# Eight products of the identity with itself, ahead of the first transposes, left out

## What is computed

```python
xn = rmsnorm(h, norm_mix_g)
proj = xn @ w_in
...
log_f = jax.nn.log_sigmoid((f_logit + b_f).astype(jnp.float32))
...
att_o = forgetting_attention(heads(q), heads(k), heads(v), log_f)
conv_o = conformer_conv(glu_in, w_dw, b_dw, ln_g, ln_b)
mixed = jnp.concatenate([att_o, conv_o], axis=-1)
h = h + mixed @ w_out
hn = rmsnorm(h, norm_ffn_g).reshape(B * T, D)
h = h + moe_ffn(hn, w_router, b_router, w_gu, b_gu, w_down, b_down).reshape(B, T, D)
return rmsnorm(h, norm_final_g)
```

## Time and profile before

| what | us |
|---|---|
| median of three executions | 1038.73 |
| lowest and highest | 1037.36, 1039.56 |
| the profiled execution's own time | 1039.37 |
| span of the profiled execution, first to last instruction | 1037.6 |
| TensorE busy | 1009.1 (97% of the span) |
| VectorE busy | 242.2 (23%) |
| ScalarE busy | 163.1 (16%) |
| mean granted TensorE clock | 0.992 |

### The profile page before, as it was taken

One profiled execution on the slowest core, in us unless ns is written; L12 is line 12 of the kernel. 1 busy time (PEld: TensorE's weight loads), 2 busy tenths in 40 slices (PEclk: granted clock), 3 DMA queues, 4 the chain that ended last, 5 costly groups with the idle time before them and its releaser, 6 DMA issues.

```text
span 1037.6 us, 11003 instructions
## 1 busy us (share of the span) xinstructions
PE 1009.1 (97%) x4821; PEld 398.1 (38%) x4822; DVE 242.2 (23%) x532; ACT 163.1 (16%) x303; POOL 15.0 (1%) x28
## 2 busy tenths in 40 slices
PE   9999999999999999999999999998999999999997
PEld 7875534333333333333333333333333333233332
DVE  3995341211011111111111112111111112011112
ACT  6144321111011111111110111010111011001102
POOL 4000000000000000000000000000000000000000
PEclk9999999999999999999999999999999999999999
DMA  9995799999999999999999999999999999999995
GB/s 310 389 421 199 277 340 400 410 416 425 428 425 436 425 435 426 433 427 431 428 436 427 432 429 430 433 431 429 430 431 426 434 429 429 427 428 426 427 421 217
DMA packets 35275, 421.62 MB, mean 406 GB/s; under 512 B 4269, under 2 KB 8665, under 8 KB 15258
## 3 DMA queue, kind: packets, MB, share of 16 engines
q1 hardware_dynamic: 33658, 420.57, 96.7%
q10 hardware_dynamic: 1568, 0.33, 0.2%
HBM read 419.82 MB, written 1.05 MB: 406 GB/s over the span
## 4 chain that ended last, share of the span: by engine, by line
PE 64%; DMA 28%; DVE 6%; ACT 1%; issue 0%; SPq 0%; DVEq 0%; ACTq 0%
PE work L1243 53%; DMA ring<-in_w_gu 24%; PE resid L1243 7%; DVE main L937 4%; DMA ring<-in_w_down 3%; PE work L1551 1%; PE work L1627 1%; DMA main<-in_x 0%; PE work L1581 0%; PE work L1362 0%; PE work L1461 0%; DVE main L944 0%; DVE ring L916 0%; DVE ring L947 0%; DVE main L991 0%
## 5 line engine op out<-in xcount | busy, mean ns | idle before, releaser
L1243 PE MATMUL work<-ring,main 128*64 128x512 f32 (+1 forms) x3080 | 689.0, 597 | 16.9 <-DMA ring<-in_w_gu 15.2
L1243 PEld LDWEIGHTS work<-ring,main 128*64 128x64 f32 (+1 forms) x3080 | 218.9, 138 | 462.3 <-issue 412.0
L1146 DVE TENSOR_SCALAR main<-work 128x512 f32<-128x512 f32 x32 | 22.1, 691 | 555.6 <-PE work L1243 555.6
L777 ACT ACTIVATE main<-main 128x512 f32<-128x512 f32 x32 | 20.2, 631 | 435.8 <-DVE main L1146 435.8
L1243 PE MATMUL work<-ring 128*128 128x256 f32 (+2 forms) x308 | 71.8, 403 | 0.9 <-DVE ring L947 0.8
L1243 PE MATMUL resid<-main 128*128 128x512 f32 (+1 forms) x136 | 68.0, 618 | 0.8 <-ACT main L840 0.8
L1243 PEld LDWEIGHTS work<-ring 128*128 128x128 f32 (+1 forms) x308 | 55.6, 186 | 15.7 <-issue 8.7
L1243 PE MATMUL work<-bgu_rows,ident 128*64 128x512 f32 (+1 forms) x260 | 61.0, 588 | 0.0
L795 ACT ACTIVATE main<-work 64x512 f32<-64x512 f32 x60 | 35.5, 591 | 126.9 <-PE work L1243 126.2
L1139 DVE TENSOR_SCALAR lent<-count,place,gates 128x64 f32<-128x64 f32 x68 | 17.9, 309 | 154.6 <-PE work L1581 146.8
L937 DVE SCALAR_TENSOR_TENSOR main<-ring,main 128x256 f32<-128x256 f32 x116 | 46.6, 478 | 1.3 <-ACT main L651 1.1
(11 more groups left out here) (200 smaller groups left out, 332.3 us busy)
## 6 DMA issues: line engine op xcount, KB each, us to landing
ring<-in_w_gu SPq DMA_DIRECT2D x33, 4096.0 KB, 40.5
ring<-in_w_gu SPq DMA_DIRECT2D x40, 2048.0 KB, 18.2
ring<-in_w_down SPq DMA_DIRECT2D x16, 4096.0 KB, 40.6
ring<-in_w_down SPq DMA_DIRECT2D x13, 2048.0 KB, 16.3
ring<-in_w_down SPq DMA_DIRECT2D x23, 1024.0 KB, 29.0
ring<-in_w_gu SPq DMA_DIRECT2D x7, 3072.0 KB, 35.8
ring<-in_w_gu SPq DMA_DIRECT2D x20, 1024.0 KB, 24.9
ring<-in_w_down SPq DMA_DIRECT2D x4, 3072.0 KB, 37.4
```

The source lines that it names most:

```text
L777: nc.scalar.activation(sig_h, gate_h, ACT.Sigmoid, scale=SWIGLU_ALPHA).then_inc(sig_ready, 1)
L1146: V.tensor_scalar(gate_h, work[:, GATE_BANK, :], SWIGLU_LIMIT, None, ALU.min).then_inc(gate_clamped, 1)
L1243: return nc.tensor.matmul(out_, lhsT, rhs, start=start, stop=stop, skip_group_check=True)
```

## The change

Both calls of `keep_warm` and the helper are left out. The eight products of `open_resid`, the transpose of `mix_rows` and everything after it stay, in the same order and with the same waits.

```diff
-            def keep_warm(n, out_):
-
-                for _ in range(n):
-                    mm(out_, ident[:, :], ident[:, :], True, True)
-
             pe.wait_ge(ident_ready, 1)
             def open_resid():
...
             open_resid()
-            keep_warm(3, work[:, 0, 0:P])
             pe.wait_ge(mix_in, 16)
             nc.tensor.transpose(work[:, 3, 0:KB], mix_rows, ident[0:KB, 0:KB]).then_inc(vecs_turned, 1)
-            keep_warm(5, work[:, 0, 0:P])
```

## The result

The changed kernel takes 1040.98 us, the median of nine executions (1039.97 to 1043.06); the kernel before, run beside it, 1038.60 (nine, 1037.17 to 1039.56). The ratio is 1.0028, 95% interval 1.0017 to 1.0038: slower, by 2.4 us in the medians. The forecast was 1040.5, inside 1038.5 to 1043.0. Of its three outcomes it had "the same" as the likeliest, with the line at 0.2%; the measured interval reaches to both sides of that line.

A forecast was written before the change was run, and what follows sets the result against it. Nothing is spare on the chain at the start (whole span: TensorE 64%, DMA 28%). A low clock until 12.3 makes the gates 1.8 us late, passed on whole: 1038.73 + 1.8 = 1040.5 us, range 1038.5 to 1043.0.

The forecast's parts named there:

- three outcomes: Whole kernel against the one before, line at 0.2%: the same 0.55, slower 0.42, faster 0.03.
- What is removed, and the pause: Before the transposes: removing 3.4 us of TensorE gains nothing; TensorE stands until 7.32, when the clock will still be low.
- The rival of an earlier start (C): At the transposes: where x lands earlier, they start sooner without the eight products; about 1038.2 us, chance 0.04.
- The rise of the clock: From the transposes on: TensorE stays at the lower level until 12.3, middle of 10.7 and 13.8; costs 1.8 us.
- its own range of 1.1 to 2.5: Loss in us for a clock rise at 10.7 (1.1) or 13.8 (2.5), that is 1039.8 to 1041.2 us.
- two other rises: Kernel before: clock rises near 6.8 after 5.2 us of work, and after 662.14 following 3.4 us of work.
- Rival A: At the start: transposes do not lift the clock, only products do; rise 16.0 to 17.8, +4.0 us, 1042.7, chance 0.23.
- The sum up to the gates: Transposes to gate products: second eight transposes 0.5 late, small ones start 1.2 late, gates 1.8 late for a rise at 12.3.
- Does it reach the end: From 15.93 to the end: the chain moves as a whole and transfers come later too, so all +1.8 us counts.
- little slack: After 80 to 85, transfers and TensorE both run nearly full: 429 GB/s, TensorE busy 50.00 of 50.00 us.
- The drop at 662.14: Late in the kernel before: clock fell to 0.50 after TensorE stood 2.1 us waiting for a transfer.

The follow-up runs named there:

- the second trace: The changed kernel run and traced again with no edit: 1041.80 us, ratio 1.0022 against the kernel before; the traced execution took 1042.39.
- lost in the loop: The kernel before with the bias products of one bank of expert 11 made five times instead of once, 3.4 us more of TensorE: ratio 0.9998.
- the kernel with transposes: The kernel before with each of the eight products replaced by two transposes of the identity: 1039.15 us, ratio 1.0005.

## Why the prediction was right, and where not

**What is removed, and the pause.** Right: nothing else moved, TensorE stands until `xn` is there (7.41), and the clock is low when it starts. The rival of an earlier start (C) gained nothing: with x landed earlier in the second trace, TensorE began at 7.11 and still lost 3.39 us.

**The rise of the clock.** This is the term that was mis-sized. I took 12.3, the middle of 10.7 and 13.8, and so 1.8 us. In five traces the rise came at 10.22, 11.21, 15.73, 16.43 and 16.62, never near the middle and only once (11.21) between the two ends: one cost (0.96 and 1.25) is below the forecast, the other (3.2 to 3.5) above its own range of 1.1 to 2.5. The bounds were the work before two other rises, 3.4 and 5.2 us. Here the transposes had run for 2.8 us before the earliest rise (7.41 to 10.22), and TensorE had worked for 9.5 before the latest (7.11 to 16.62). That the median, +2.4, lies inside the forecast's own range is luck: of the five traced costs one does, and the median lies between the two kinds.

**Late rise: nearly the price, for the wrong reason.** Rival A priced a rise between 16.0 and 17.8 at 3.6 to 4.5 us; three traces show a rise at 15.7 to 16.6 and 3.2 to 3.5, a little under it. But its reason, that transposes do not lift the clock, falls with the two traces of the changed kernel in which the clock rises after transposes alone (10.22 and 11.21). What holds the clock down in the other three is open. Between 10.7 and about 13 they do the small transposes and the 32-column gates; no run here takes these apart from the moment at which the transposes began.

**The sum up to the gates.** For a rise at 10.7 I had the gates 1.1 late; with a rise at 10.22 they are 0.97 late. For a late rise I had them 1.9 late. They are 1.20 late in the second trace (11.84), where the transposes began at 7.11, and 1.55 in the one with the rise at 15.73 (12.19), where they began at 7.45. The nine small transposes, which I put at 1.6 to 1.8 us at the lower level, take 1.13 in both (10.71 to 11.84 in the second). The rest of the second trace's loss is in the gate and `glu_a` products: from 11.84 to 19.2 instead of 10.64 to 15.8, 2.2 us, inside what rival A's working allows for them (1.0 and 0.7 to 1.6).

**Does it reach the end.** Right, and now shown with a slope of 1.02. The reasons hold too: the ring is full, the releases come late, the loads with them. What I did not see is that the path has a twin on TensorE (the earlier trace rows show only the longer one), and that the same microseconds lost in the loop cost nothing: there TensorE was 4.8 us behind at 616 and the transfers were not, so "little slack" held for the transfers alone.

## What to carry to other kernels

TensorE standing idle before its first long work can be paid for later: read how long one record of a known shape takes at the start and a little later, and look at more than one trace, since the rise of the clock, and with it the cost, differs from one execution to the next. Ask of every delay on which side of the last stall of the transfers it falls: 1 to 3.5 us lost before it went to the end whole, 3.4 us lost in the loop behind it vanished. And a chain that ended last can hide a second one almost as long: a loss common to both is paid, and a gain on one is worth no more than the difference between them.

## What the runs showed of the hardware that was not expected

The clock fell in a stretch in which TensorE never stood. In the first trace of the changed kernel, TensorE by shape from 258.9 to 262.8, then the stretches before and behind 262.81 (us, busy, granted clock, DMA share, GB/s):

```profile
L1243 PE MATMUL resid<-spare,lent 32*128 32x512 f32 x8 | 3.7, 600 | 0.0
```

```profile
259.39:262.81 3.42, 3.42 (x11) 1.00 0.99 422
262.81:266.22 3.41, 3.41 (x12) 0.50 1.03 437
```

TensorE is busy all the time, mostly with products that use 32 of the 128 rows, and then the clock is 0.50 for 3.41 us. The drop at 662.14 had 2.1 us of standing before it, which the prediction took for its cause; a drop without standing shows that there are others, and which one acts here is open. In the kernel with transposes the same place shows 0.50 for 6.8 us, and both traces of the kernel before show no drop there, with the same products.

Up to the first record of a rise the column of the granted clock prints 1.00, in the changed kernel as in the earlier trace rows, although the transposes start 0.21 us apart there: before the first rise the durations tell the level, not the column.
